# Expert loop: VectorE makes the one-hots two pairs ahead instead of one, and ahead of splitting a pair's result

## The chip, the cores and the metric

One core of a Trainium2 chip runs the whole program in one launch. The metric is the device time of one execution in microseconds (us); the time before is the median of three runs. Five engines work side by side, each from its own list of instructions, and wait for one another by semaphores only: TensorE (PE in the profile; its weight loads are PEld), VectorE (DVE), ScalarE (ACT), GpSimd (POOL) and SyncE (SP, which here issues nearly all loads).

## The reference, cut to what matters

A trunk of two layers works on 256 tokens (128 of a prompt, 128 of a sample) of 1024 values. Each layer is a token mixer (a gated recurrence in the first, neighbourhood attention in the second) followed by a mixture of experts, and this mixture is what the change touches:

```
scores = sigmoid(x @ w_router)                       # 256 tokens x 64 experts
eidx   = 6 experts of each token, chosen by groups;  combine = their normalised weights, 0 elsewhere
hid    = silu(x @ w_gate[e]) * (x @ w_up[e])         # each of 64 experts, 1024 -> 256
routed = sum over e of (hid * combine[:, e]) @ w_down[e]
out    = routed + shared expert of the same form
```

All numbers are float32. The weights of one layer's experts are 64 x 3 matrices of 1024 x 256.

## The kernel before, in words

The experts are taken in pairs, 32 pairs to a layer, and each expert has 64 slots for its tokens, so that a pair fills the 128 rows of the array. For a pair, VectorE makes a *one-hot* (`one_hots`, line 1032): for each of the 256 tokens a row of 128 zeros with a one where the token has its slot, found by comparing the token's rank in the expert with a row of slot numbers. TensorE multiplies the tokens (held as three bf16 parts) by this one-hot (`gather`, lines 1492 to 1505), which collects the pair's tokens; it also turns the one-hot and reads the slots' weights (`turn_hots`). Then `gate_up` (1527) multiplies by the gate and up weights, ScalarE takes the silu (line 676), VectorE forms `hid` (line 1114), TensorE transposes it (line 1551), multiplies by the down weights (`down`, 1543), and the result is put back to the tokens by the turned one-hot (`combine`, 1518), one pair later.

Before that, a pair's result is split into three bf16 parts, in two halves. For each half ScalarE copies the first part (`y_high`), VectorE subtracts it from the result in PSUM (`y_rest`, line 1121), ScalarE copies the second part (`y_mid`), and VectorE subtracts again (line 1126, `y_low`). The results of `down` lie in PSUM banks 6 and 7, a half in each, and the next `gather` writes into the same banks: it waits for `y_rest` of the pair before.

Each engine's order is written out by hand, and each takes its list strictly in that order. On TensorE a pair's turn is, counted from the end of `gate_up(n)`: `gather(n+1)`, transposes of `hid(n)`, `combine(n-1)`, `turn_hots(n+1)`, the two halves of down(n), `gate_up(n+1)`. On VectorE it is `pair_step` (1107): `one_hots` for pair n+1, `hid(n)`, the second half of the gathered tokens of n+1 (`gathered`, line 1105; ScalarE copies the first half), then the splitting of the result of n. VectorE can so make the one-hot of n+1 only when it has done with the splitting of n-1. Both lists are loops over two pairs with one step ahead of the loop and one behind it (`experts_pass`, lines 1129 and 1571). There are two rooms for everything that is held per pair (`onehot[:, j]`, `hid[:, j]`, the weights' ring), with j = n mod 2.

The gate and up weights of pair n+2 are loaded by SP when `gate_up(n)` has ended (line 370), and its down weights when the second half of down(n) has ended (line 375). In the first pair of a layer the shared expert is worked on in between, and that pair's one-hot is made in `experts_front`. A further pass over the experts for those with more than 64 tokens exists in the code and has no instructions in this trace.

Of the kernel before, what the change touches and what calls it, by code (L numbers as in the profile page):

```python
# [36 lines left out]
E, TOP_K, GROUPS, TOP_GROUPS = 64, 6, 8, 4  # L37
F = 256
SLOTS = 64
PAIRS = E // 2  # L40
# [31 lines left out]
def build(nc, io):  # L72
    ctx = ExitStack()
    with ctx:
# [710 lines left out]
        def _(dve):  # L785
# [240 lines left out]
            def one_hots(M, r, expert, j):  # L1026

                base = C_IOTA + r * SLOTS
                shape = (P, 2, 2, SLOTS)
                slots = (consts[:, base:base + SLOTS] if isinstance(base, int) else consts[:, bass.ds(base, SLOTS)])  # L1030
                ranks = rank[:, :, bass.ds(expert, 2)] if not isinstance(expert, int) else rank[:, :, expert:expert + 2]
                dve.tensor_tensor(onehot[:, j].rearrange("p a (e s) -> p a e s", e=2),  # L1032
                                  slots.unsqueeze(1).unsqueeze(1).broadcast_to(shape),
                                  ranks.unsqueeze(3).broadcast_to(shape), ALU.is_equal).then_inc(M.onehot, 1)
# [68 lines left out]
            def gathered(M, n, j):  # L1103
                dve.wait_ge(M.xg_ps[1], n + 1)
                dve.tensor_copy(xg[:, j, 4:8], psum[:, 7, :].rearrange("p (k t) -> p k t", t=P)).then_inc(M.xg[1], 1)  # L1105

            def pair_step(M, r, n, j, next_expert):

                if next_expert is not None:

                    one_hots(M, r, next_expert, 1 - j)
                dve.wait_ge(M.silu, n + 1)
                dve.wait_ge(M.hot_t, n + 1)
                dve.scalar_tensor_tensor(out=hid[:, j], in0=silu[:, j], scalar=slot_w[:, j:j + 1],  # L1114
                                         in1=psum[:, 4, F:2 * F], op0=ALU.mult, op1=ALU.mult).then_inc(M.hid, 1)
                if next_expert is not None:
                    gathered(M, n + 1, 1 - j)
                for half in range(2):
                    dve.wait_ge(M.y_high, n * 2 + (half + 1))
                    ps = slice(half * (P // 2), (half + 1) * (P // 2))  # L1120
                    dve.tensor_tensor(y_rest[:, :, ps].rearrange("s k p -> s p k"),  # L1121
                                      psum[:, 6 + half, :].rearrange("s (p k) -> s p k", k=K),
                                      y[:, j, 0, :, ps].rearrange("s k p -> s p k"), ALU.subtract).then_inc(M.y_rest, 1)
                    dve.wait_ge(M.y_rest, n * 2 + (half + 3))
                    dve.wait_ge(M.y_mid, n * 2 + (half + 1))
                    ins = dve.tensor_tensor(y[:, j, 2, :, ps], y_rest[:, :, ps], y[:, j, 1, :, ps], ALU.subtract)  # L1126
                ins.then_inc(M.y_low, 1)

            def experts_pass(M, r):
                if not isinstance(r, int):  # L1130
                    one_hots(M, r, 0, 0)
                gathered(M, r * PAIRS, 0)
                pair_step(M, r, r * PAIRS, 0, 2)
                with dve.Fori(0, PAIRS // 2 - 1) as h:  # L1134
                    for i in (1, 2):
                        pair_step(M, r, r * PAIRS + h * 2 + i, i % 2, h * 4 + 2 * (i + 1))
                pair_step(M, r, r * PAIRS + PAIRS - 1, 1, None)

            def experts(m):
                M = moe[m]  # L1140
                dve.wait_ge(M.table, 1)
                experts_pass(M, 0)
                more = dve.value_load(extra[0:1, 0:1].bitcast(I32), min_val=0, max_val=3)
                with dve.If(more > 0):
                    with dve.Fori(0, more) as r:
                        experts_pass(M, r + 1)

                def added(k):
                    if k % 2 == 0:
                        dve.wait_ge(M.done, k // 2 + 1)  # L1150

                residual(mod[:, m, 5], added)
# [573 lines left out]
```

## Time and profile before

| what | before |
|---|---|
| median of 3 runs | 1752.52 us (1752.44 to 1754.31) |
| span of the profiled execution, first to last instruction | 1752.8 us |
| PE busy | 1607.8 us, 92% |
| ACT busy | 698.3 us, 40% |
| DVE busy | 518.0 us, 30% |
| DMA, mean over the span | 291 GB/s |

The profile gives no time for the profiled execution beyond its span. A core's span is divided among engines that work at the same time, so the shares don't add up to one. The first layer's expert loop lies at about 390 to 960 us of the span and the second layer's at about 1160 to 1720 us; within them all views repeat themselves with each pair. An engine's idle time ahead of an instruction is put down to what released that instruction, which is written behind an arrow.

### The profile page before, as it was taken

What the parts mean: (1) busy time and instruction counts of PE and PEld (TensorE: products, weight loads), DVE (VectorE), ACT (ScalarE), POOL (GpSimd) and SP (SyncE); (2) the same over time, 40 slices, a digit from 0 to 9 for tenths busy, and PEclk for the clock granted to TensorE, in tenths of its full rate; (3) what the DMA queues carried; (4) which work ended last, traced back from release to release, by engine and by line L of the source; (5) the groups of instructions that cost most, each with busy time, mean ns of one, the idle gap of its engine ahead of it and who ended that gap; (6) DMA issues with size and microseconds to landing.
All of it is one profiled execution on the core that took longest, in us unless ns stands there. A gap on an engine that the chain in (4) does not pass through costs nothing.

```text
span 1752.8 us, 30448 instructions
## 1 busy us (share of the span) xinstructions
PE 1607.8 (92%) x13039; PEld 1131.2 (65%) x13039; DVE 518.0 (30%) x857; ACT 698.3 (40%) x1055; POOL 18.6 (1%) x25
## 2 busy tenths in 40 slices
PE   5999999989999999999997998999999999999995
PEld 3767766856666666666665776866666666666663
DVE  1034044151222223232323216232222223232324
ACT  2213322233454545454544204225454545454444
POOL 0000000010000000000000000010000000000000
PEclk8999888989999999999998999899999999999998
DMA  9967566546999999999998333438999999999970
GB/s 315 323 227 266 193 251 240 204 168 272 354 370 357 366 358 365 359 358 367 354 370 301 87 118 156 186 126 320 356 368 359 354 365 363 364 358 366 353 286 25
DMA packets 130113, 510.50 MB, mean 291 GB/s; under 512 B 11257, under 2 KB 19601, under 8 KB 97297
## 3 DMA queue, kind: packets, MB, share of 16 engines
q1 hardware_dynamic: 124832, 506.23, 75.9%
q10 hardware_dynamic: 5232, 3.57, 0.7%
q8 instruction: 37, 0.61, 0.1%
q14 instruction: 12, 0.09, 0.0%
HBM read 506.64 MB, written 3.15 MB: 291 GB/s over the span
## 4 chain that ended last, share of the span: by engine, by line
PE 58%; ACT 23%; DVE 12%; issue 5%; DMA 1%; DVEq 1%; ACTq 0%
PE psum L1230 57%; ACT arena L503 22%; DVE arena L1121 8%; DVE arena L1032 1%; PE psum L1551 1%; DMA arena<-in_moe_router_bias 1%; DVE arena L803 0%; DVE arena L1126 0%; ACT arena L526 0%; DVE arena L845 0%; ACTq L500 0%; DVEq L1134 0%; ACT arena L744 0%; ACT L514 0%; PE psum L1698 0%
## 5 line engine op out<-in xcount | busy, mean ns | idle before, releaser
L1230 PE MATMUL psum<-arena 128*64 128x256 f32 (+9 forms) x12756 | 1577.3, 348 | 112.9 <-DVE arena L1032 63.7
L1230 PEld LDWEIGHTS psum<-arena 128*64 128x64 f32 (+3 forms) x12756 | 1100.9, 136 | 582.4 <-issue 347.1
L503 ACT ACTIVATE arena<-psum 128x512 f32<-128x512 f32 (+4 forms) x514 | 455.7, 903 | 573.8 <-PE psum L1230 468.0
L1121 DVE TENSOR_TENSOR arena<-psum,arena 128x512 f32<-128x512 f32 x128 | 137.7, 1076 | 523.8 <-ACT arena L503 523.8
L503 ACT ACTIVATE arena<-arena 128x512 bf16<-128x512 f32 (+1 forms) x144 | 88.6, 625 | 148.8 <-DVE arena L1121 146.2
L1126 DVE TENSOR_TENSOR arena<-arena 128x512 bf16<-128x512 f32 x128 | 88.7, 693 | 101.1 <-ACT arena L503 101.1
L1105 DVE COPY arena<-psum 128x512 f32<-128x512 f32 x64 | 44.3, 693 | 182.4 <-PE psum L1230 182.4
L825 DVE TENSOR_TENSOR arena<-psum,arena 128x16 f32<-128x16 f32 x12 | 2.1, 175 | 144.4 <-PE psum L1230 144.4
L510 ACT ACTIVATE arena<-arena 128x512 f32<-128x512 f32 x20 | 12.3, 629 | 73.6 <-DVE arena L845 73.6
L845 DVE SCALAR_TENSOR_TENSOR arena<-psum,arena 128x128 f32<-128x128 f32 x64 | 17.8, 343 | 65.6 <-PE psum L1230 65.6
L676 ACT ACTIVATE arena<-psum 128x256 f32<-128x256 f32 x64 | 24.7, 386 | 30.0 <-PE psum L1230 30.0
L1114 DVE SCALAR_TENSOR_TENSOR arena<-arena,psum 128x256 f32<-128x256 f32 x64 | 30.4, 476 | 16.5 <-ACT arena L676 16.5
L560 ACT ACTIVATE arena<-psum 128x1024 f32<-128x1024 f32 x8 | 8.2, 1026 | 57.3 <-PE psum L1230 57.3
L492 POOL TENSOR_TENSOR arena<-arena 128x512 f32<-128x512 f32 (+1 forms) x16 | 16.9, 1091 | 1129.6 <-ACT arena L503 1129.6
L1551 PE MATMUL psum<-arena 128*128 128x128 f32 x128 | 25.0, 277 | 2.1 <-DVE arena L1114 2.1
L1032 DVE TENSOR_TENSOR arena<-arena 128x256 bf16<-128x256 f32 x64 | 26.8, 418 | 0.0
L503 ACT ACTIVATION_READ_ACCUMULATOR arena<-psum 64x1 f32 x128 | 25.1, 196 | 0.8
L526 ACT ACTIVATE arena<-arena 128x128 f32<-128x128 f32 x32 | 12.8, 481 | 12.4 <-DVE arena L805 7.8
L1551 PEld LDWEIGHTS psum<-arena 128*128 128x128 f32 x128 | 13.0, 142 | 3.0 <-DVE arena L1114 3.0
L926 DVE TENSOR_TENSOR arena<-arena 128x1024 f32<-128x1024 f32 x12 | 14.1, 1220 | 0.1
L605 ACT ACTIVATE arena<-arena 128x1024 f32<-128x1024 f32 x4 | 4.2, 1059 | 23.3 <-DVE arena L898 23.3
L575 ACT ACTIVATE arena<-arena 128x512 f32<-128x512 f32 x8 | 5.1, 641 | 20.1 <-DVE arena L926 20.1
(137 smaller groups left out, 309.6 us busy)
## 6 DMA issues: line engine op xcount, KB each, us to landing
arena<-in_moe_w_gate SPq DMA_DIRECT2D x64, 2048.0 KB, 7.9
arena<-in_moe_w_up SPq DMA_DIRECT2D x64, 2048.0 KB, 12.6
arena<-in_moe_w_down SPq DMA_DIRECT2D x64, 2048.0 KB, 9.3
arena<-in_ada_w SPq DMA_DIRECT2D x24, 2048.0 KB, 15.1
arena<-in_hgrn_w_in SPq DMA_DIRECT2D x10, 2048.0 KB, 13.5
arena<-in_na_w_qkv SPq DMA_DIRECT2D x6, 2048.0 KB, 18.1
arena<-in_hgrn_w_out SPq DMA_DIRECT2D x1, 4096.0 KB, 12.6
arena<-in_na_w_o SPq DMA_DIRECT2D x1, 4096.0 KB, 13.7
```

The source lines that it names most:

```text
L492: pool.tensor_tensor(out, h_rest[:, a, ks], h_tok[:, part, a, ks], ALU.subtract)\
L503: return act.activation(out, in_, ACT.Copy, **kw)
L676: act.activation(silu[:, j], psum[:, 4, 0:F], ACT.Silu).then_inc(M.silu, 1)
L845: ins = dve.scalar_tensor_tensor(out=xT[:, k, at], in0=psum[:, k // 2, (k % 2) * NT + s * T:(k % 2) * NT + (s + 1) * T], scalar=g[:, k, s: ...
L926: ins = dve.tensor_tensor(dif[d].rearrange("p u (b t) -> p (u b) t", t=size), view, view[:, :, at:at + 1].broadcast_to(shape), ALU.subtract)
L1032: dve.tensor_tensor(onehot[:, j].rearrange("p a (e s) -> p a e s", e=2), slots.unsqueeze(1).unsqueeze(1).broadcast_to(shape), ranks.unsque ...
L1105: dve.tensor_copy(xg[:, j, 4:8], psum[:, 7, :].rearrange("p (k t) -> p k t", t=P)).then_inc(M.xg[1], 1)
L1114: dve.scalar_tensor_tensor(out=hid[:, j], in0=silu[:, j], scalar=slot_w[:, j:j + 1], in1=psum[:, 4, F:2 * F], op0=ALU.mult, op1=ALU.mult). ...
L1121: dve.tensor_tensor(y_rest[:, :, ps].rearrange("s k p -> s p k"), psum[:, 6 + half, :].rearrange("s (p k) -> s p k", k=K), y[:, j, 0, :, p ...
L1126: ins = dve.tensor_tensor(y[:, j, 2, :, ps], y_rest[:, :, ps], y[:, j, 1, :, ps], ALU.subtract)
L1230: return pe.matmul(out, lhsT, rhs, start=start, stop=stop, skip_group_check=True, **kw)
L1551: ins = pe.transpose(psum[:, 5, c * P:(c + 1) * P], hid[:, j, c * P:(c + 1) * P], ident)
```

## The change

VectorE's list alone changes. The one-hot is made two pairs ahead, behind `hid` and the copy of the gathered tokens, and ahead of the splitting of the same pair's result; the one-hot of pair 1 is made at the start of the pass. It goes into the room that the one-hot of pair n has left. The loop is one turn shorter, and two more steps are written out behind it.

```
-            def pair_step(M, r, n, j, next_expert):
-
-                if next_expert is not None:
-
-                    one_hots(M, r, next_expert, 1 - j)
+            def pair_step(M, r, n, j, later_expert, last=False):
+
                 dve.wait_ge(M.silu, n + 1)
                 dve.wait_ge(M.hot_t, n + 1)
                 dve.scalar_tensor_tensor(out=hid[:, j], in0=silu[:, j], scalar=slot_w[:, j:j + 1],
                                          in1=psum[:, 4, F:2 * F], op0=ALU.mult, op1=ALU.mult).then_inc(M.hid, 1)
-                if next_expert is not None:
+                if not last:
                     gathered(M, n + 1, 1 - j)
+                if later_expert is not None:
+                    one_hots(M, r, later_expert, j)
                 for half in range(2):
                     dve.wait_ge(M.y_high, n * 2 + (half + 1))
...
             def experts_pass(M, r):
                 if not isinstance(r, int):
                     one_hots(M, r, 0, 0)
+                one_hots(M, r, 2, 1)
                 gathered(M, r * PAIRS, 0)
-                pair_step(M, r, r * PAIRS, 0, 2)
-                with dve.Fori(0, PAIRS // 2 - 1) as h:
+                pair_step(M, r, r * PAIRS, 0, 4)
+                with dve.Fori(0, PAIRS // 2 - 2) as h:
                     for i in (1, 2):
-                        pair_step(M, r, r * PAIRS + h * 2 + i, i % 2, h * 4 + 2 * (i + 1))
-                pair_step(M, r, r * PAIRS + PAIRS - 1, 1, None)
+                        pair_step(M, r, r * PAIRS + h * 2 + i, i % 2, h * 4 + 2 * (i + 2))
+                pair_step(M, r, r * PAIRS + PAIRS - 3, 1, E - 2)
+                pair_step(M, r, r * PAIRS + PAIRS - 2, 0, None)
+                pair_step(M, r, r * PAIRS + PAIRS - 1, 1, None, last=True)
```

## Rows read from the trace of the kernel before

**Rows 1.** The page: busy us (share of the span), instructions; then GB/s in 40 slices.

```profile
PE 1607.8 (92%) x13039; PEld 1131.2 (65%) x13039; DVE 518.0 (30%) x857; ACT 698.3 (40%) x1055; POOL 18.6 (1%) x25
GB/s 315 323 227 266 193 251 240 204 168 272 354 370 357 366 358 365 359 358 367 354 370 301 87 118 156 186 126 320 356 368 359 354 365 363 364 358 366 353 286 25
```

**Rows 2.** Waits of PE, whole span: waiter, releaser: us in total, times, longest.

```profile
PE psum L1230 <- DVE arena L1032: 63.7, 60, 1.1
```

**Rows 3.** Stretch of one pair: length; busy us (instructions) by engine; clock, DMA share, GB/s.

```profile
805.29:822.69 17.40, 16.35 (x158) 11.08 (x158) 4.95 (x8) 8.35 (x12) 0.00 (x0) 1.00 0.94 371
```

**Rows 4.** Timeline at a pair's border: start us, us, engine, line, operation; idle, releaser.

```profile
816.60 1.09 DVE L1121 TENSOR_TENSOR arena<-psum,arena 128x512 f32<-128x512 f32 x1 [6.66 <-ACT arena L503]
...
820.74 1.06 DVE L1121 TENSOR_TENSOR arena<-psum,arena 128x512 f32<-128x512 f32 x1 [1.58 <-ACT arena L503]
...
822.58 0.69 DVE L1126 TENSOR_TENSOR arena<-arena 128x512 bf16<-128x512 f32 x1 [0.78 <-ACT arena L503]
822.73 0.39 ACT L676 ACTIVATE arena<-psum 128x256 f32<-128x256 f32 x1 [0.26 <-PE psum L1230]
...
823.19 0.42 DVE L1032 TENSOR_TENSOR arena<-arena 128x256 bf16<-128x256 f32 x1
...
823.52 0.47 DVE L1114 SCALAR_TENSOR_TENSOR arena<-arena,psum 128x256 f32<-128x256 f32 x1
...
823.74 2.87 PE L1230 MATMUL psum<-arena 128*128 128x128 bf16 x48 [1.05 <-DVE arena L1032]
825.29 0.60 ACT L503 ACTIVATE arena<-psum 128x512 f32<-128x512 f32 x1 [2.18 <-PE psum L1230]
...
826.44 0.39 PE L1551 MATMUL psum<-arena 128*128 128x128 f32 x2
...
826.64 0.69 DVE L1105 COPY arena<-psum 128x512 f32<-128x512 f32 x1 [2.65 <-PE psum L1230]
```

**Rows 5.** Chain of waits at the same border: start us, us, what.

```profile
823.62 0.12 issue
```

**Rows 6.** Timeline of a pass's last pair, which has no one-hot ahead of hid.

```profile
944.43 0.69 DVE L1126 TENSOR_TENSOR arena<-arena 128x512 bf16<-128x512 f32 x1 [0.77 <-ACT arena L503]
944.57 0.39 ACT L676 ACTIVATE arena<-psum 128x256 f32<-128x256 f32 x1 [0.25 <-PE psum L1230]
945.04 0.48 DVE L1114 SCALAR_TENSOR_TENSOR arena<-arena,psum 128x256 f32<-128x256 f32 x1
```

**Rows 7.** Timeline at a pass's start: PE (shared expert's tail, first gather), then VectorE.

```profile
380.26 11.10 PE L1230 MATMUL psum<-arena 128*128 128x64 f32 x78 [0.91 <-DVE arena L1070]
...
391.32 0.69 DVE L1105 COPY arena<-psum 128x512 f32<-128x512 f32 x1 [1.92 <-PE psum L1230]
```

**Rows 8.** PE's loop branch (line 1585), 440 to 500 us; a gather behind it, 455 to 460.

```profile
L1585 PEldq COMPARE_BRANCH  x2: 220/228/237, 454.9 to 489.7; - x2
...
458.17 2.02 PE L1230 MATMUL psum<-arena 128*128 128x128 bf16 x33 [1.07 <-DVE arena L1032]
```

**Rows 9.** DMA issues: KB each, us to landing; then the up weights', 500 to 900 us.

```profile
arena<-in_moe_w_gate SPq DMA_DIRECT2D x64, 2048.0 KB, 7.9
arena<-in_moe_w_up SPq DMA_DIRECT2D x64, 2048.0 KB, 12.6
arena<-in_moe_w_down SPq DMA_DIRECT2D x64, 2048.0 KB, 9.3
...
DMA to landing us min/median/max: 12.0/12.2/14.6
```

**Rows 10.** Stretches of one pair (columns as in rows 3), then of a wait behind the pass.

```profile
822.69:823.69 1.00, 0.00 (x0) 0.00 (x0) 1.00 (x3) 0.39 (x1) 0.00 (x0) 1.00 0.20 78
...
827.69:833.69 6.00, 6.00 (x45) 3.29 (x44) 0.00 (x0) 3.08 (x6) 0.00 (x0) 1.00 1.00 423
...
958.90:966.00 7.10, 6.35 (x29) 4.77 (x30) 5.08 (x17) 1.89 (x3) 0.00 (x0) 0.54 0.02 4
```

## The prediction

> **What bounds the kernel now.** I read the page's engine shares first: TensorE is busy for 92% of the span, and no other engine comes near that [rows 1]. So the time lies in TensorE's work and in what it waits for. The list of waits, read for TensorE alone, names one wait that repeats: 60 times it waited for the one-hot (line 1032), 63.7 us in total and never over 1.1 us [rows 2]. That is 30 pairs in each of two layers and 1.06 us a time.
>
> The stretch of one pair says the same from the other side: 17.40 us long, TensorE busy for 16.35, granted clock 1.00 [rows 3]. The 1.05 us left is one hole, and the timeline shows its place. The gather begins at 823.74 with 1.05 us idle before it, so gate_up ended at 822.69; ScalarE's silu, released by that end, starts at 822.73 [rows 4]. Why the one-hot is late is read backward from it: VectorE makes it at 823.19 to 823.61, right behind the last subtraction of the splitting (line 1126, from 822.58), and that stands behind the second y_rest (820.74 to 821.80). The one-hot needs none of this data. It only stands behind it in VectorE's list. From its end to the gather is another 0.12 us [rows 5].
>
> **The change part by part.**
>
> *The one-hot leaves this place.* From pair 2 on it is made one pair earlier, so its wait is over before TensorE comes to it. The gather has one other wait, for the y_rest of the bank that it overwrites. The second y_rest ends at 821.80, and it is the gather's second half that needs it: 0.89 us before gate_up's end, and before that half's start by more [rows 4]. So the gather would start when gate_up ends, and the hole closes: 60 x 1.06 = 63.7 us, the total in the list of waits [rows 2].
>
> *What is late next?* Behind the gather TensorE transposes hid. Where no one-hot stands ahead of it, hid starts 0.61 us after the last subtraction's start (945.04 against 944.43) and 0.08 us after the silu's end, and it takes 0.48 [rows 6]. Put on the border of rows 4, that is 822.58 + 0.61 + 0.48 = 823.67, or 0.98 us after gate_up's end. The transposes come 2.70 us after the gather's start (826.44 - 823.74), so 1.72 us are left [rows 4]. The combine needs the last subtraction, which ends at 823.27, later still. ScalarE's silu has 0.26 us of idle time before it, so ScalarE is not late either. Everything behind the gather keeps its place relative to the gather, and I find no second hole.
>
> *Does a hole remain between gate_up and the gather?* The trace has no such border without a wait inside the loop. The nearest row is the pass's start, where float32 products of the shared expert are followed by the first bf16 gather: TensorE's run from 380.26 goes on for 11.10 us through both, with no idle time shown [rows 7]. So I take 0. The other end is the 0.12 us between a releaser and the gather [rows 5], 60 x 0.12 = 7.2 us. Below zero I allow 0.04 us a pair, the delay from gate_up's end to the silu, in case the engine's modelled end is early: 2.4 us [rows 4]. TensorE's loop branch loses the cover of the hole in half of the pairs. It takes at most 0.24 us, and one stands at 454.9, while the gather behind it starts at 458.17 after 1.07 us idle, so gate_up ended at 457.10: the branch is over about 2 us ahead of that [rows 8]. It costs nothing.
>
> *The one-hot's new place.* It costs 0.42 us [rows 4], 30 times in a layer. It now follows the copy of the gathered tokens, which ends at 826.64 + 0.69 = 827.33. VectorE then waits 6.66 us in each pair for the first y_rest, as its idle time shows [rows 4], and the one-hot lies inside that. Without this cover it would be 0.42 us a pair in front of the splitting, 25 us in all. The one-hot of pair 1 is now made ahead of the first gathered copy, where VectorE is idle for 1.92 us [rows 7]: again nothing. No one-hot is added or dropped. The room that it writes was last read by turn_hots, whose results hid's own wait already covers, so no wait is added and no DMA is moved past anything; SP's list is as it was. Two more steps written out behind the loop are VectorE's instructions in the same order; hid's spare 1.72 us covers small delays there.
>
> *The DMA.* A shorter pair asks more of it. A pair's loads are three of 2048 KB, 6.29 MB [rows 9]: 362 GB/s at 17.40 us and 385 at 16.35. The DMA isn't full now: for six microseconds of a pair it moves 423 GB/s, and for one at the border 78 [rows 10]. At 423 the loads need 14.9 us, under 16.35. There is room in time as well: the up weights are on SP's list right after gate_up(n) and land 12.2 us later in the median, 14.6 at most [rows 9], and gate_up(n+2) lies a pair and more behind.
>
> By the Trainium skill (page "DMA: Bandwidth & Descriptors", section "Where 436 GB/s comes from") loads from HBM are bound by the HBM side, at about 358 GB/s for a core. By that rule the loop would stand at its bound already and the change would give nothing. The trace doesn't agree: it has 371 GB/s over a pair and 423 over six microseconds, and no wait of TensorE for weights in the loop.
>
> **The sum.** It is made against the profiled execution, whose span is 1752.8 us; no other time is shown for it, and the median of the runs is 1752.5, so the two may stand for each other. 1752.5 - 63.7 = 1688.8 us, 3.6% less. Its own range, from the two ends above, is 1686 to 1696.
>
> **The rivals.**
>
> *The loads become the bound.* If the DMA can't go beyond what its best slice of the page shows, 373 GB/s [rows 1], a pair takes 6.29 / 0.373 = 16.87 us and the gain is 0.53 x 60 = 32 us: 1721. If it can't go beyond the 362 that it moves now, the wait for the one-hot becomes one for weights and the time stays 1752.5. For it: the DMA's busy share is 0.94 over a pair [rows 3], and all slices of the loops lie between 354 and 373. Against it: the 423, the empty microsecond, and the early landing. The part-way case gets 6%, no gain at all 4%.
>
> *The wait only moves.* If TensorE is held by the splitting's last subtraction, which ends 0.58 us after gate_up's end (822.58 + 0.69 = 823.27), 0.47 us a pair are gained, 28 us: 1724. The code lets only the combine wait for it, and that comes 2.9 us later. 4%.
>
> *Slower: TensorE's clock.* The gain holds at a granted clock of 1.00. If the denser work were given less over the loops, a pair would take 16.35 divided by the clock: at 0.94 that is 17.39 and the gain is gone, and below it the kernel is slower. At 0.90 it would be 18.17 us, 60 x 0.77 = 46 us more: 1799. For it: nothing in the loops is run without holes so far. Against it: the low grant that I find, 0.54, comes behind a wait (958.90 to 966.00) [rows 10], not behind dense work. 3%.
>
> **How the numbers follow.** The forecast gets 83%, the rivals 6, 4, 4 and 3. The range for 8 in 10 is the likeliest case's own with a little above it for a part of the DMA case, which shares its side: 1685 to 1702. A measurement of this kernel can tell about 0.2% (3.5 us) from no change. Faster by over that: 83 + 6 + 4 = 93%; within it 4%; slower 3%.
>
> **What would show it.** In the profile after, the wait of TensorE for line 1032 is gone from the list or down to a few, and a pair's stretch is 16.35 to 16.5 us long with TensorE busy throughout. The one-hot stands behind line 1105, about 3.6 us after gate_up's end. The transposes start without idle time, but for each pass's last pair, which has no gather ahead of them. The DMA shows about 385 GB/s in the loops. It would be wrong if the hole stayed with another releaser (line 1121, 1126 or 1114), if TensorE waited for the weights' loads, or if the clock fell below 1.00 in the loops.

## The result, and the profile after

The changed kernel takes 1685.5 us (median of 4 runs, 1682.7 to 1686.8) against 1752.5, a ratio of 0.9613 (95% interval 0.9600 to 0.9627): 67.0 us less, where 63.7 were forecast. The profiled execution's span is 1684.9 us, 67.9 less than before.

The page of the changed kernel, with the lines that answer to [rows 1], and under them its chain of waits by engine and by line:

```profile
PE 1604.5 (95%) x13039; PEld 1132.3 (67%) x13039; DVE 517.7 (31%) x857; ACT 697.9 (41%) x1055; POOL 18.6 (1%) x25
...
GB/s 324 323 230 276 180 300 182 238 223 150 382 379 388 387 391 384 380 384 389 392 378 349 50 163 162 93 133 324 390 383 392 387 377 393 386 385 379 393 293 26
...
PE 92%; DVE 3%; ACT 3%; DMA 1%; issue 1%; ACTq 0%; DVEq 0%
PE psum L1232 90%; ACT arena L503 2%; PE psum L1553 1%; DMA arena<-in_moe_router_bias 1%; DVE arena L803 0%; ACT arena L526 0%; ACTq L500 0%; DVE arena L1065 0%; DVE arena L1120 0%; ACT arena L744 0%; PE psum L1700 0%; DVE arena L805 0%; ACT L514 0%; DVE arena L1200 0%; PE psum L1670 0%
```

Two lines were added, so lines behind the change have new numbers (TensorE's 1230 is 1232 here, the transposes' 1551 is 1553, the subtractions' 1121 and 1126 are 1120 and 1125). TensorE's busy time is nearly what it was; the span is shorter, and TensorE alone now makes 92% of the chain that ended last (58% on the page before). The loops load at 377 to 393 GB/s in a slice.

The waits of TensorE in the changed kernel (waiter, releaser: us in total, times, longest), which answer to [rows 2]:

```profile
PE psum L1232 <- DVE arena L1125: 14.9, 2, 7.4
PE psum L1232 <- ACT arena L526: 14.3, 5, 4.1
PE psum L1232 <- ACT arena L503: 10.9, 15, 1.1
...
PE psum L1553 <- DVE arena L1111: 2.1, 2, 1.0
```

The 60 waits for the one-hot are gone, and none with as many times has come in their place. Two stretches of one pair (columns as in [rows 3]):

```profile
811.32:827.60 16.28, 16.28 (x160) 11.09 (x161) 4.95 (x8) 8.34 (x12) 0.00 (x0) 1.00 0.99 394
827.60:843.88 16.28, 16.28 (x160) 11.09 (x160) 4.97 (x8) 8.33 (x12) 0.00 (x0) 1.00 0.97 383
```

A pair takes 16.28 us, with TensorE busy throughout at a granted clock of 1.00. That is 1.12 us less than before and not 1.05: the busy time itself is 0.07 shorter. The timeline at a pair's border, in answer to [rows 4]:

```profile
821.51 1.09 DVE L1120 TENSOR_TENSOR arena<-psum,arena 128x512 f32<-128x512 f32 x1 [6.33 <-ACT arena L503]
...
825.65 1.06 DVE L1120 TENSOR_TENSOR arena<-psum,arena 128x512 f32<-128x512 f32 x1 [1.59 <-ACT arena L503]
...
827.49 0.69 DVE L1125 TENSOR_TENSOR arena<-arena 128x512 bf16<-128x512 f32 x1 [0.78 <-ACT arena L503]
827.52 2.70 PEld L1232 LDWEIGHTS psum<-arena 128*128 128x128 bf16 x48 [0.39 <-issue]
827.64 0.39 ACT L676 ACTIVATE arena<-psum 128x256 f32<-128x256 f32 x1 [0.25 <-PE psum L1232]
...
828.10 0.47 DVE L1111 SCALAR_TENSOR_TENSOR arena<-arena,psum 128x256 f32<-128x256 f32 x1
...
829.09 0.60 ACT L503 ACTIVATE arena<-psum 128x512 f32<-128x512 f32 x1 [1.06 <-PE psum L1232]
...
830.24 0.39 PE L1553 MATMUL psum<-arena 128*128 128x128 f32 x2
...
830.44 0.69 DVE L1105 COPY arena<-psum 128x512 f32<-128x512 f32 x1 [1.86 <-PE psum L1232]
...
831.05 0.42 DVE L1032 TENSOR_TENSOR arena<-arena 128x256 bf16<-128x256 f32 x1
```

The silu starts at 827.64, so gate_up ended at 827.60 by the 0.04 us of before. The gather's first weight load starts at 827.52, 0.08 us *ahead* of that end. hid ends at 828.57 and is needed at 830.24. The one-hot stands at 831.05, behind the gathered copy, and VectorE's idle time ahead of the first y_rest has shrunk from 6.66 to 6.33 us.

### The profile page after: what moved, and what is told of

Its sections match the earlier page's. It is cut to its first block, busy times and chain, and to the rows that moved or that the text cites. A ratio compares the mean times of both kernels' runs of the same rounds, so it can differ in the third digit from the quotient of the medians.

```text
span 1684.9 us, 30416 instructions
## 1 busy us (share of the span) xinstructions
PE 1604.5 (95%) x13039; PEld 1132.3 (67%) x13039; DVE 517.7 (31%) x857; ACT 697.9 (41%) x1055; POOL 18.6 (1%) x25
## 4 chain that ended last, share of the span: by engine, by line
PE 92%; DVE 3%; ACT 3%; DMA 1%; issue 1%; ACTq 0%; DVEq 0%
PE psum L1232 90%; ACT arena L503 2%; PE psum L1553 1%; DMA arena<-in_moe_router_bias 1%; DVE arena L803 0%; ACT arena L526 0%; ACTq L500 0%; DVE arena L1065 0%; DVE arena L1120 0%; ACT arena L744 0%; PE psum L1700 0%; DVE arena L805 0%; ACT L514 0%; DVE arena L1200 0%; PE psum L1670 0%
## 5 line engine op out<-in xcount | busy, mean ns | idle before, releaser
L1232 PE MATMUL psum<-arena 128*64 128x256 f32 (+9 forms) x12756 | 1574.0, 348 | 50.7 <-DVE arena L1125 14.9
L492 POOL TENSOR_TENSOR arena<-arena 128x512 f32<-128x512 f32 (+1 forms) x16 | 16.9, 1090 | 1095.5 <-ACT arena L503 1095.4
## 6 DMA issues: line engine op xcount, KB each, us to landing
arena<-in_moe_w_up SPq DMA_DIRECT2D x64, 2048.0 KB, 14.3
arena<-in_na_w_o SPq DMA_DIRECT2D x1, 4096.0 KB, 14.3
```

What stands on the lines that cost most here:

```text
L492: pool.tensor_tensor(out, h_rest[:, a, ks], h_tok[:, part, a, ks], ALU.subtract)\
L1232: return pe.matmul(out, lhsT, rhs, start=start, stop=stop, skip_group_check=True, **kw)
```

## The experiments

One quantity is used in most of them: the length of an expert pass, from the first start of a transpose to the last in a layer, which holds 30 borders with a one-hot. It leaves out the kernel's front, which varies from run to run (the first start lies between 406.6 and 410.6 us in the traces here), and what lies between and behind the passes. It is read from the transposes' line, first and last start, here for the kernel before and the changed one:

```profile
L1551 PE MATMUL psum<-arena x64: 272/275/329, 410.6 to 945.7; 128*128 128x128 f32 x64
...
L1551 PE MATMUL psum<-arena x64: 272/275/327, 1181.6 to 1716.8; 128*128 128x128 f32 x64
```

```profile
L1553 PE MATMUL psum<-arena x64: 272/276/328, 408.9 to 910.2; 128*128 128x128 f32 x64
...
L1553 PE MATMUL psum<-arena x64: 272/276/328, 1146.9 to 1648.2; 128*128 128x128 f32 x64
```

Both layers together are 1070.3 us before and 1002.6 after: 67.7 us, so nearly the whole gain lies in the loops. (Outside them the front is 1.7 us shorter in the changed kernel's trace and the rest 1.5 us longer, which cancels to 0.2.) The list of waits gave 63.7, and 4.0 us are to be explained.

**The changed kernel again, as a base (twice).** No edit.

> The changed kernel once more, as the base for the others of this group. Both theories: 1683 to 1687 us. Theory A: the time beyond the closed hole (67 us gained where the list of waits gave 63.7) sits at the border of gate_up and gather, about 0.065 us in each of 60 pairs, because the gather's first weight load now runs under gate_up's last products. Theory B: it sits elsewhere (the kernel's front, the loads, the splitting), and a wait costs the length of its hole and no more.

> The changed kernel as the base of this group: 1683 to 1688 us.

Measured: 1687.8 us (1686.4 to 1688.8, ratio 0.9625, interval 0.9612 to 0.9638) and 1687.1 us (1685.6 to 1689.0, ratio 0.9617, interval 0.9604 to 0.9630). The first is 0.8 us above the upper end that I had set. The passes have the same length as above within 0.1 us.

**The one-hot behind the splitting.**

```
                 if not last:
                     gathered(M, n + 1, 1 - j)
-                if later_expert is not None:
-                    one_hots(M, r, later_expert, j)
                 for half in range(2):
...
                 ins.then_inc(M.y_low, 1)
+                if later_expert is not None:
+                    one_hots(M, r, later_expert, j)
```

> One-hots still two pairs ahead, but behind the splitting of a pair's result, where they stood before. Theory (the lead is what counts): the gather doesn't wait, hid comes 0.34 us later and is still early by over 1 us, so the time is that of the changed kernel within 3 us. Rival (the place ahead of the splitting is needed too, as hid comes late): 0.34 us in each of 60 pairs, 20 us more than the changed kernel.

Measured: 1753.3 us, ratio 0.9997 (0.9988 to 1.0006): all of the gain is gone, and neither expectation holds. TensorE waits for the one-hot as before, and VectorE's timeline at a border shows why:

```profile
PE psum L1232 <- DVE arena L1032: 63.5, 60, 1.1
```

```profile
821.66 0.69 DVE L1123 TENSOR_TENSOR arena<-arena 128x512 bf16<-128x512 f32 x1 [0.77 <-ACT arena L503]
822.27 0.42 DVE L1032 TENSOR_TENSOR arena<-arena 128x256 bf16<-128x256 f32 x1
822.61 0.48 DVE L1111 SCALAR_TENSOR_TENSOR arena<-arena,psum 128x256 f32<-128x256 f32 x1
```

My expectation had miscounted. The end of one pair's step and the start of the next are the same place in VectorE's list, so this kernel has the order of before under another name: last subtraction, one-hot, hid. "Two pairs ahead" is no lead of its own; it is how the code says that the one-hot stands ahead of the splitting. As a control the run shows that the shorter loop, the written-out steps and the argument's new count are worth nothing.

**A wait for the last subtraction.** All else is the changed kernel.

```
                 if next_expert is not None:
+                    if not first:
+                        pe.wait_ge(M.y_low, n)
                     gather(M, n + 1, n, 1 - j)
```

> The changed kernel with one wait more: each gather but a layer's first two also waits for the last subtraction of the splitting, which ends 0.57 us after gate_up. This is the rival of a wait that only moves. Hole about 0.62 us in 60 pairs. Theory A: 0.62 + 0.065 a pair, 41 us more than the changed kernel. Theory B: 37 us more.

Measured: 1738.7 us, ratio 0.9914 (0.9901 to 0.9928), 51 us above the base, where 37 or 41 were expected. (The prediction had priced its rival of a wait that only moves at 1724 us.) The holes are longer than I had worked out: 64.6 less the 14.9 that are in the changed kernel too, 49.7 us or 0.83 in each of 60.

```profile
PE psum L1232 <- DVE arena L1125: 64.6, 62, 7.4
```

```profile
L1555 PE MATMUL psum<-arena x64: 272/275/328, 408.4 to 936.5; 128*128 128x128 f32 x64
...
L1555 PE MATMUL psum<-arena x64: 272/275/327, 1172.6 to 1700.8; 128*128 128x128 f32 x64
```

The passes are 1056.3 us, 53.7 more than the changed kernel's: 4.0 beyond the holes, as theory A has it.

**A wait for gate_up's own end.** The same edit with another semaphore.

```
+                    if not first:
+                        pe.wait_ge(M.gu, n + 1)
                     gather(M, n + 1, n, 1 - j)
```

> The changed kernel with one wait more: each gather but a layer's first two waits for the end of the gate_up just ahead of it, so that nothing of the gather can start under it. Hole of 0.04 to 0.10 us. Theory A: 0.065 us more than the hole, 6 to 10 us more than the changed kernel over 60 pairs. Theory B: 2 to 6 us more.

Measured: 1704.8 us, ratio 0.9721 (0.9708 to 0.9735), 17 us above the base. Again the hole was longer than expected, 0.25 us and not 0.04 to 0.10:

```profile
PE psum L1232 <- PE psum L1232: 15.0, 60, 0.3
```

```profile
L1555 PE MATMUL psum<-arena x64: 272/275/329, 407.7 to 918.5; 128*128 128x128 f32 x64
...
L1555 PE MATMUL psum<-arena x64: 272/275/327, 1153.1 to 1663.9; 128*128 128x128 f32 x64
```

The passes are 1021.6 us, 19.0 more than the changed kernel's, and 4.0 beyond the holes. The whole time is up by less because, in its trace, the first transposes start at 407.7 us instead of the base's 410.2, and the stretch between the passes is 234.6 us instead of 236.7.

**hid ahead of the one-hot, in the kernel before.**

```
-                if next_expert is not None:
-                    one_hots(M, r, next_expert, 1 - j)
                 dve.wait_ge(M.silu, n + 1)
...
                 if next_expert is not None:
+                    one_hots(M, r, next_expert, 1 - j)
                     gathered(M, n + 1, 1 - j)
```

> The kernel before with hid made ahead of the one-hot, still one pair ahead: the one-hot ends about 0.33 us later. If TensorE's hole sets the time, its 60 holes grow from 1.06 to about 1.4 us and the time by 20 us, to 1772 us, and a pass's length is that of the changed kernel plus the holes plus 0.067 us a border. Rival (VectorE's hid was the true bound and the one-hot only stood in its way): no slower than before, 1745 to 1753 us.

Measured: 1777.0 us, ratio 1.0126 (1.0111 to 1.0142), 22 us slower than before. The holes are 87.4 us, 1.46 each, and the passes 1094.0 us, 91.4 more than the changed kernel's and once more 4.0 beyond the holes:

```profile
PE psum L1228 <- DVE arena L1032: 87.4, 60, 1.5
```

```profile
L1549 PE MATMUL psum<-arena x64: 272/275/330, 409.5 to 956.5; 128*128 128x128 f32 x64
...
L1549 PE MATMUL psum<-arena x64: 272/276/329, 1192.2 to 1739.2; 128*128 128x128 f32 x64
```

Together, over 60 borders:

| kernel | both passes, us | more than the changed kernel | TensorE's holes | beyond the holes |
|---|---|---|---|---|
| changed | 1002.6 | | 0 | |
| wait for gate_up's end | 1021.6 | 19.0 | 15.0 | 4.0 |
| wait for the last subtraction | 1056.3 | 53.7 | 49.7 | 4.0 |
| before | 1070.3 | 67.7 | 63.7 | 4.0 |
| hid ahead of the one-hot | 1094.0 | 91.4 | 87.4 | 4.0 |

In these four kernels a hole of 0.25 to 1.46 us costs itself and 0.067 us more, whatever its length. Theory B, by which the 4 us lie elsewhere, falls: in the kernel with the wait for gate_up's end neither VectorE's order nor the loads' list differs from the changed kernel's, and the 4.0 are there. Theory A has the place right; whether its cause, the weight load, is right too is taken up in the next section.

**One bf16 part instead of three.** The gathers and combines multiply the first part alone.

```
-                            for part in range(3):
+                            for part in range(1):
...
-                                         onehot[:, j, a], a == 0 and part == 0, a == 1 and part == 2)
+                                         onehot[:, j, a], a == 0 and part == 0, a == 1 and part == 0)
...
-                    for part in range(3):
+                    for part in range(1):
```

> The changed kernel with less work for TensorE: gather and combine multiply only the first of the three bf16 parts, so 32 of 48 products of each gather and 16 of 24 of each combine are left out (the output loses those parts). TensorE's work of a pair falls by about 1.8 + 1.75 us to 12.7 us. What bounds the pair then? Theory: the loads, at the 423 GB/s that they reach inside a pair: 14.9 us. Rival, loads bound at the 373 GB/s of the best slice of before: 16.9 us; at 362 GB/s: 17.4 us. If the loads can do more than 423, 12.7 to 14.5 us.

Measured: 1587.0 us, ratio 0.9044 (0.9028 to 0.9061). TensorE now waits for weights, and the loads run without a break (stretch of 300 us, columns as in [rows 3]; then the wait):

```profile
500.00:800.00 300.00, 262.62 (x2170) 155.87 (x2169) 100.10 (x140) 166.23 (x239) 0.00 (x0) 0.99 1.02 417
```

```profile
PE psum L1232 <- DMA arena<-in_moe_w_up: 91.8, 51, 1.9
```

417 GB/s over 300 us is 6.29 / 0.417 = 15.1 us for a pair, close to the 14.9 of the theory; the rivals' 16.9 and 17.4 fall. VectorE's hid agrees: its starts lie 15.08 us apart there, and 13.0 us in the first pairs, before TensorE waits for weights. By the Trainium skill (page "DMA: Bandwidth & Descriptors", section "Where 436 GB/s comes from") about 358 GB/s bind a core's loads from HBM. On this core, running alone, they don't: the measured 417 decides.

**The last combine but one, moved into the wait behind the pass.**

```
-                if not first:
+                if not first and next_expert is not None:
                     pe.wait_ge(M.y_low, n)
                     combine(M, 1 - j)
...
                     ins.then_inc(M.y_ps[half], 1)
+                if next_expert is None:
+                    pe.wait_ge(M.y_low, n)
+                    combine(M, 1 - j)
```

> The changed kernel with the combine of each layer's last pair but one moved behind the last pair's down products, into the 7.4 us in which TensorE waits for the last splitting. It takes 2.6 us out of the line ahead of that wait, and gives back about 0.9 us of waiting for the transposed hid that it covered: 1.7 us a layer, 3.4 us in all. If the shorter hole also keeps TensorE's clock from falling behind it, up to 4 us a layer more: 3 to 12 us below the changed kernel. Rival: the splitting, not TensorE, sets the end and starts as late as now: no gain.

Measured: 1682.1 us, ratio 0.9581 (0.9568 to 0.9594), beside 1687.1 and 0.9617 (0.9604 to 0.9630) for the changed kernel on the same chip: 5.0 us less, inside the 3 to 12 expected. TensorE's timeline behind the first layer's last transposes, in this kernel and then in the base:

```profile
911.98 6.38 PE L1232 MATMUL psum<-arena 128*64 128x512 f32 x40 [0.47 <-ACT arena L503]
923.54 7.93 PE L1232 MATMUL psum<-arena 128*128 128x256 bf16 x40 [5.18 <-DVE arena L1125]
```

```profile
910.73 6.37 PE L1232 MATMUL psum<-arena 128*128 128x256 bf16 x40
924.53 8.86 PE L1232 MATMUL psum<-arena 128*128 128x256 bf16 x40 [7.44 <-DVE arena L1125]
```

The wait falls from 7.44 to 5.18 us, one of 0.47 appears where the combine had covered it, and the products behind the wait take 7.93 us instead of 8.86, with a mean granted clock of 0.78 over them instead of 0.70. The rival falls: the last splitting's first subtraction starts 5.38 us after the last transposes' start, 7.46 us in the base, so the splitting did start earlier. Of the kernels here that keep all three parts, this is the fastest.

## What the prediction had right, and the step that failed

*What bounds the kernel.* Right. The holes alone order the five kernels of the table, and lengthening them by moving hid ahead of the one-hot cost 22 us.

*The one-hot leaves its place, and what is late next.* Right. No wait of TensorE took the place of the 60. hid ends 0.97 us after gate_up's end, where 0.98 was worked out, and 1.67 us ahead of the transposes. The transposes keep 2.1 us of waiting, once in each pass's last pair. The one-hot stands 3.45 us after gate_up's end (3.6 forecast), inside VectorE's idle time.

*"Does a hole remain between gate_up and the gather?"* This is the step that failed. I took 0 and allowed at most 0.04 us a pair below it. It came out 0.067 us below in each of 60 borders: a gather that has to wait costs more than the hole shown in front of it. So the term of 63.7 us is 63.7 + 60 x 0.067 = 67.7, and the allowance of 2.4 us had to be 4.0. With the measured ratio the time is 1684.7 us on the forecast's base (1682 to 1687), just under the range's lower end of 1685. The two repeats, at 1686.8 and 1685.4 us on that base, lie just above it, so the range was missed by little; the term was off all the same.

Where the 0.067 lies can be read from single products at the border. These are the last two of gate_up and the first two of the gather in the changed kernel:

```profile
827.21 0.38 PE L1232 MATMUL psum<-arena 128*64 128x256 f32 x2
827.53 0.29 PE L1232 MATMUL psum<-arena 128*128 128x128 bf16 x2
```

TensorE's products are pipelined (the gather's start about 0.056 us apart, and each is shown as 0.22 us long), and the profile models their ends. gate_up's last product ends at 827.59 by the model, and the gather's first one starts before that, at 827.53. At each of the 60 borders it starts 0.067 us (0.067 to 0.068) ahead of that end, read from the unrounded trace. From its start to the transposes is 2.71 us, against 2.70 before [rows 4], so the whole gather has moved by that much. A shown hole begins only at the modelled end and leaves out the 0.067 us of overlap that an unbroken run of products has. Whether the two products really overlap or the model puts the end late, the traces don't say; the time is the same.

The trace of the kernel before held such an overlap. At the pass's start, where I read "no idle time" from [rows 7], the shared expert's last product ends at 388.52 by the model, and the gather's first starts at 388.36:

```profile
387.93 0.59 PE L1230 MATMUL psum<-arena 128*128 128x512 f32 x1
388.36 0.39 PE L1230 MATMUL psum<-arena 128*128 128x128 bf16 x4
```

That is 0.16 us, with another product in front, so the size depends on the products. No idle time is not yet an overlap of 0: the starts have to be read. My reason for the 0.04 us had the wrong sign, too. An end that is modelled too early makes the real hole shorter and the gain smaller; an end that lies behind the next product's possible start makes the gain larger.

A weight load hidden under gate_up, which I suspected after the result, is not the cause. By the Trainium skill (page "TensorE: Matmul & The Clock Gate", section "Architectural detail: the array is 16× 32×32, not 1× 128×128") TensorE's queue can draw a weight load ahead of products that still run. The trace after agrees, as the gather's first load starts 0.07 us ahead of gate_up's modelled end. But the gather's first product follows its load within 0.01 us in both kernels (823.73 and 823.74 before, 827.52 and 827.53 after), so the 0.067 us is not the time of a load that is hidden now and wasn't before.

*The loads.* Right, and with less to spare than the early landings suggested. The up weights land 14.3 us after their issue instead of 12.2:

```profile
DMA to landing us min/median/max: 12.9/14.3/14.8
```

The loop draws 383 to 394 GB/s and waits for none of it. The run with one part puts the end at 417 GB/s, or 15.1 us a pair, so 1.2 us of a pair are left before the loads bind. The rival by which they bound already is out. One reading of that rival was wrong: in the loops' whole slices the best is 370 GB/s and the lowest 353 [rows 1], not 373 and 354, so its part-way price was 6.29 / 0.370 = 17.0 us a pair and 1728 us. The forecast doesn't rest on it.

*The clock.* It stays at 1.00 in the loops, as forecast.

Some of my expectations after the result were wrong as well. The run with the one-hot behind the splitting had the order of before, which I didn't see. And the holes of the two added waits were worked out too short: a gather released by gate_up's own end came 0.25 us after it, one released by the last subtraction 0.83 us after gate_up. The releases take 0.12 us in [rows 5]; why they take more in those two kernels is left open.

## What to carry to other kernels

Look at what the instruction in a repeating wait really needs: here nothing, it only stood behind other work in its engine's list, and moving it in front of that work gave the whole hole. Count the places in the list and not the names of the steps, since the end of one turn and the start of the next are one place. And to the hole in front of a waiting product add the overlap with the product ahead that an unbroken run would have, here 0.067 us a time.

## What the runs showed of the hardware that I had not expected

A wait of TensorE at this border cost 0.067 us beyond the idle time shown, and the same 4.0 us in 60 whether the holes were 0.25, 0.83, 1.06 or 1.46 us long: without a wait the next product starts that much ahead of the modelled end of the one before it. Waiting for TensorE's own end made a hole of 0.25 us. And the loads of one core ran at 417 GB/s for 300 us on end.
